# The first norm's rows loaded once and spread by products, scale ahead of shift, and two bias rows moved behind the experts

## The reference

```python
c_act = jax.nn.silu(c)
mod = c_act @ ada_w[l] + ada_b[l]                 # 1024 -> 6144
shift1, scale1, gate1, shift2, scale2, gate2 = jnp.split(mod, N_MOD, axis=-1)
h = modulate(rmsnorm(x, norm1_g[l]), shift1, scale1)   # h * (1 + scale) + shift
proj = h @ w_in[l]
...
out = peer(h2, ...)      # 128 gathered rows of each table for every token
...
p = h @ w_in_2 + b_in_2  # second block; the two gates' columns of b_in_2 are 1024 each
```

## Time and profile before

| | us |
|---|---|
| median of three runs | 1439.09 (1437.6 to 1442.28) |
| the profiled execution's own time | 1438.15 |
| its span | 1436.4 |
| PE busy | 1252.2 (87%) |
| DVE busy | 770.3 (54%) |
| POOL busy | 522.6 (36%) |
| ACT busy | 412.8 (29%) |

### The profile page before, as it was taken

The page is one execution under the profiler, slowest core; times in us unless marked ns, Lnnn a source line. Parts: engine busy times, 40 slices in busy tenths (PEclk is TensorE's granted clock), DMA queues, the critical chain, the costliest instruction groups (busy, mean ns, idle before and its releaser), DMA issues.

```text
span 1436.4 us, 13292 instructions
## 1 busy us (share of the span) xinstructions
PE 1252.2 (87%) x4187; PEld 653.2 (45%) x4187; DVE 770.3 (54%) x1584; ACT 412.8 (29%) x1106; POOL 522.6 (36%) x578
## 2 busy tenths in 40 slices
PE   3899879999777777777987777999999999999997
PEld 0486546555222222222543222654444446887443
DVE  1437258557356575878667678477996522110003
ACT  2122224334324343343434434322115211111000
POOL 1000036666457777777777777001111000000000
PEclk9899989999979999999999999999999999999999
DMA  9786369999999999999999999243334343434430
GB/s 352 269 299 234 117 222 391 406 406 408 401 403 409 410 409 410 409 407 406 409 402 407 405 406 405 85 162 117 117 118 155 110 158 118 176 129 164 163 129 29
DMA packets 131117, 399.85 MB, mean 278 GB/s; under 512 B 10328, under 2 KB 11480, under 8 KB 130664
## 3 DMA queue, kind: packets, MB, share of 16 engines
q0 software_dynamic: 74448, 271.09, 47.8%
q1 hardware_dynamic: 54448, 121.18, 23.4%
q10 hardware_dynamic: 2152, 6.74, 1.3%
HBM read 397.92 MB, written 1.05 MB: 278 GB/s over the span
## 4 chain that ended last, share of the span: by engine, by line
PE 48%; DMA 24%; DVE 9%; POOL 8%; issue 4%; DVEq 3%; ACT 2%; SPq 1%; ACTq 1%; POOLq 0%
PE psum L579 27%; DMA gathered<-in_peer_u_dram,expert_idx 20%; PE psum L1074 8%; PE psum L824 7%; POOL gathered L496 4%; POOL gathered L510 4%; DVE work L1494 3%; DMA gathered<-in_peer_v_dram,expert_idx 2%; DVE gathered L1831 2%; DMA gathered<-in_ada_w_dram 2%; PE psum L662 1%; PE psum L602 1%; DVE work L2116 1%; PE psum L1049 1%; SPq L426 1%
## 5 line engine op out<-in xcount | busy, mean ns | idle before, releaser
L824 PE MATMUL psum<-gathered,modr 128*128 128x512 f32 x1024 | 506.5, 627 | 127.1 <-DMA gathered<-in_peer_v_dram,expert_idx 104.8
L1831 DVE CUSTOM_DVE_ANT_0 gathered<-gathered,psum 128x1024 f32<-128x1024 f32 x256 | 312.1, 1219 | 173.2 <-DMA gathered<-in_peer_u_dram,expert_idx 171.1
L824 PEld LDWEIGHTS psum<-gathered,modr 128*128 128x128 f32 x1024 | 182.2, 194 | 431.7 <-DMA gathered<-in_peer_v_dram,expert_idx 249.1
L496 POOL DMA_INDIRECT gathered<-in_peer_u_dram,expert_idx x256 | 252.7, 987 | 312.1 <-DVE expert_idx L1502 182.3
L510 POOL DMA_INDIRECT gathered<-in_peer_v_dram,expert_idx x256 | 240.2, 938 | 85.1 <-issue 70.0
L579 PE MATMUL psum<-featT,weight_ring 128*128 128x256 f32 (+2 forms) x1280 | 221.5, 332 | 1.6 <-ACT featT L1112 1.4
L579 PEld LDWEIGHTS psum<-featT,weight_ring 128*128 128x128 f32 x1280 | 200.7, 194 | 32.0 <-issue 13.7
L579 PE MATMUL psum<-weight_ring,featT 128*128 128x512 f32 (+1 forms) x480 | 207.9, 588 | 2.4 <-ACT featT L1112 2.4
L1494 DVE TENSOR_TENSOR work<-work 128x1088 f32<-128x1088 f32 (+5 forms) x115 | 118.1, 1042 | 129.2 <-ACT work L1141 101.1
L579 PEld LDWEIGHTS psum<-weight_ring,featT 128*128 128x128 f32 x480 | 90.1, 192 | 108.4 <-issue 104.3
L1273 ACT ACTIVATE gel<-dots 128x1 f32<-128x1 f32 x256 | 51.3, 200 | 276.1 <-DVEq L1833 275.8
(11 more groups left out here) (283 smaller groups left out, 884.9 us busy)
## 6 DMA issues: line engine op xcount, KB each, us to landing
weight_ring<-in_w_in_dram SPq DMA_DIRECT2D x13, 2048.0 KB, 8.9
weight_ring<-in_ada_w_dram SPq DMA_DIRECT2D x11, 2048.0 KB, 17.2
weight_ring<-in_w_up_dram SPq DMA_DIRECT2D x8, 2048.0 KB, 8.8
weight_ring<-in_w_down_dram SPq DMA_DIRECT2D x8, 2048.0 KB, 7.8
weight_ring<-in_peer_wq_dram SPq DMA_DIRECT2D x4, 2048.0 KB, 14.7
gathered<-in_w_in_dram SPq DMA_DIRECT2D x2, 2048.0 KB, 12.9
gathered<-in_peer_u_dram,expert_idx POOLq DMA_INDIRECT x256, 11.2
gathered<-in_peer_v_dram,expert_idx POOLq DMA_INDIRECT x256, 11.2
```

The lines of the kernel that those rows point to most:

```text
L496: pool.indirect_dma_start(u_rows[:, slot, :], None, T["peer_u"], bass.IndirectOffsetOnAxis(ap=expert_idx[:, r % 2, k:k + 1], axis=0),).the ...
L824: mm = pe.matmul(psum[:, SUM_BANK + half, :], diag[:, e % 8, :], v_rows[:, slot, 512 * half:512 * (half + 1)], start=(e % EXPERTS == 0), s ...
L1831: dve.tensor_tensor_reduce(u_rows[:, slot, :], u_rows[:, slot, :], h2_rows[t], 1.0, 0.0, ALU.mult, ALU.add, dots[:, col:col + 1])
```

## The change

- The two broadcast loads of the head become loads of one row each (8 KB of `ada_b`, 4 KB of `norm1_g`) into partition 0, on the same queue and at the same places in its order.
- PE spreads them: after the first chunk's product, two products of one row (`ones[0:1, :]` by the `norm1_g` row) fill two PSUM banks, and DVE copies these 1024 columns to `A1`. Four more (`ada_bias`) write the bias into the four banks of the sums, and `ada_sum_on_bias(i)` adds its sum on top.
- The chunks come in the order 2, 3, 0, 1, so the scale is there first. DVE makes the gain of one half straight from PSUM, then that half of `x * rs * A1` for both tiles, then the same for the other half. When a shift bank is full, DVE adds that half from PSUM, for tile 0 and then for tile 1. `h1_ready` counts four halves, and PE's turns wait each for its own half.
- SP issues the bias rows GS0 and GM0 not while experts are gathered but with V0 and O0, behind the wait for `h0_ready`.

The diff, cut to these:

```diff
@@ plan
-    ada(0, 4)
+    ada(2, 4)
+    ada(0, 2)
@@ SP
                     sp.dma_start(bc_raw, T["s5_bc"]).then_inc(flag("in_bc"), 16)
-                    for i, lo in ((2, GS0), (3, GM0)):
-                        sp.dma_start(vec[:, D * i:D * (i + 1)], rowvec("b_in_2", lo, lo + D)).then_inc(
-                            flag("in_bias2"), 16)
                 if c == LAST_ADA + 4:
                     sp.wait_ge(flag("h0_ready"), TT)
-                    for i, lo in ((0, V0), (1, O0)):
+                    for i, lo in ((0, V0), (1, O0), (2, GS0), (3, GM0)):
@@ PE
-            ada(0)
-            for i in range(1, 4):
-                ada(i)
-                ada_sum(i - 1)
-            ada_sum(3)
+            def ada_bias(i):
+                pe.matmul(bank_of("ada", i), ones[0:1, :], modr[0:1, 512 * i:512 * (i + 1)],
+                          start=True, stop=False)
+            def ada_sum_on_bias(i):
+                turn_read_wait(pe, "ada", i, 0)
+                pe.matmul(bank_of("ada", i), quarter_rows[:, :], ada_part[:, i % 2, :], start=False,
+                          stop=True).then_inc(bank_full[GROUP_BANK[("ada", i)]], 1)
+            ada(2)
+            pe.wait_ge(flag("in_mod"), 32)
+            for half in range(2):
+                last = pe.matmul(psum[:, 6 + half, :], ones[0:1, :], A1[0:1, 512 * half:512 * (half + 1)],
+                                 start=True, stop=True)
+            last.then_inc(flag("gain_full"), 1)
+            for i in ADA_ORDER[:4]:
+                ada_bias(i)
+            ada(3)
+            ada_sum_on_bias(2)
+            ada(0)
+            ada_sum_on_bias(3)
+            ada(1)
+            ada_sum_on_bias(0)
+            ada_sum_on_bias(1)
...
+            def turn_h1(t):
+                for q in range(2):
+                    bank = begin_turn("h1", t, q)
+                    pe.wait_ge(flag("h1_ready"), TT * q + t + 1)
@@ ACT
-            load(modr[:, 0:2 * D], rowvec("ada_b", 0, 2 * D), "in_mod")
+            load(modr[0:1, 0:2 * D], T["ada_b"][0:2 * D].partition_broadcast(1), "in_mod")
             load(pos_i[:, :], T["positions"], "in_pos")
-            load(A1, rowvec("norm1_g", 0, D), "in_n1")
+            load(A1[0:1, :], T["norm1_g"][0:D].partition_broadcast(1), "in_mod")
@@ DVE
-            dve.wait_ge(flag("in_n1"), 16)
-            for i in range(4):
-                add_mod(i)
-                if i >= 2:
-                    dve.drain()
-                    sl = slice(512 * (i - 2), 512 * (i - 1))
-                    stt(A1[:, sl], scale1[:, sl], 1.0, A1[:, sl], ALU.add, ALU.mult)
+            dve.wait_ge(flag("gain_full"), 1)
+            dve.tensor_copy(A1, psum[:, 6:8, :].rearrange("p b n -> p (b n)"))
             dve.drain()
+            for half in range(2):
+                sl = slice(512 * half, 512 * (half + 1))
+                group_wait(dve, "ada", 2 + half)
+                read_out(stt(A1[:, sl], bank_of("ada", 2 + half), 1.0, A1[:, sl], ALU.add, ALU.mult),
+                         "ada", 2 + half)
+                dve.drain()
+                for t in range(TT):
+                    stt(hbuf[:, t, sl], xres[:, t, sl], rs[:, t:t + 1], A1[:, sl], ALU.mult, ALU.mult)
+            for half in range(2):
+                sl = slice(512 * half, 512 * (half + 1))
+                group_wait(dve, "ada", half)
+                dve.drain()
+                tt(hbuf[:, 0, sl], hbuf[:, 0, sl], bank_of("ada", half), ALU.add).then_inc(
+                    flag("h1_ready"), 1)
+                read_out(tt(hbuf[:, 1, sl], hbuf[:, 1, sl], bank_of("ada", half), ALU.add), "ada", half)
+                dve.drain().then_inc(flag("h1_ready"), 1)
-            for t in range(TT):
-                modulated(t, A1, shift1, "h1_ready")
```

More of the change, by code:

```diff
@@ L71 @@
 ADA_AT = {52: 10, 56: 11}
-ADA_ORDER = (0, 1, 2, 3, 4, 5, 8, 9, 6, 7, 10, 11)
+ADA_ORDER = (2, 3, 0, 1, 4, 5, 8, 9, 6, 7, 10, 11)
 PACK = [("c", KD), ("conv_w", 3 * CT), ("conv_g", CT), ("b_uqk", 12), ("qk_w", 32), ("qk_b", 8),
@@ L355, in build @@
             s5c[:, i, :] for i in range(15))
-        turns = [("ada", i, 0) for i in range(4)]
+        turns = [("ada", i, 0) for i in ADA_ORDER[:4]]
         turns += [("h1", t, q) for t in range(TT) for q in range(2)]
@@ L613, in _ @@
             pe.wait_ge(flag("consts"), 1)
+            def ada_bias(i):
[15 more added lines that the diff above has]
+            ada_sum_on_bias(2)
             ada(0)
-            for i in range(1, 4):
-                ada(i)
-                ada_sum(i - 1)
-            ada_sum(3)
+            ada_sum_on_bias(3)
+            ada(1)
+            ada_sum_on_bias(0)
+            ada_sum_on_bias(1)
             def tile_by_tile(name, src, ready, products, turn=None, before=None):
                 w = {}
-                units = 1 if turn else 2
+                units = 2
                 def tile(t):
@@ L669, in first_chunk @@
                         turn_read_wait(pe, name, 1, 1)
-            tile_by_tile("h1", hbuf, "h1_ready", [("q1", lambda t: t, 512), ("kv1", lambda t: t, 256)])
+            def turn_h1(t):
+                for q in range(2):
+                    bank = begin_turn("h1", t, q)
+                    pe.wait_ge(flag("h1_ready"), TT * q + t + 1)
+                    for j in range(4):
+                        k = 4 * q + j
+                        last = pe.transpose(bank[:, j * P:(j + 1) * P], hbuf[:, t, k * P:(k + 1) * P],
+                                            ident[:, :])
+                    last.then_inc(turned, 1)
+            tile_by_tile("h1", hbuf, "h1_ready", turn=turn_h1, products=[("q1", lambda t: t, 512), ("kv1", lambda t: t, 256)])
             def turn_rotated(t):
@@ L1546, in add_mod @@
                 group_wait(dve, "ada", i)
-                if i == 0:
-                    dve.wait_ge(flag("in_mod"), 16)
                 if i == 4:
```

## The result

The changed kernel takes 1425.87 us (median of 6 runs, 1423.99 to 1430.23) beside 1439.7 us of the kernel before in the same session (6 runs, 1437.6 to 1442.28): the ratio is 0.9904 with an interval of 0.9888 to 0.992. So it is faster, by 0.8 to 1.1%. The forecast was 1425.3 us with a range of 1421.5 to 1432.0, and the chance for "faster" was 0.9. A repeat in a later session, told at the end of the experiments, gave 1432.1 us, 0.1 us outside the range; what makes the kernel's own runs differ by so much is the most useful thing that this case showed.

The account below looks back on a forecast made before the run. The head was taken as bound by DMA bytes, then a serial stretch, and the experts by DMA. Terms 8.8 + 2.4 + 2.6 = 13.8 us off the median of 1439.1 gave 1425.3 us, range 1421.5 to 1432.0.

Parts of the forecast that it names:

- Bytes of the head: Head loads: 1.56 MB fewer at 389 GB/s land the last ada_w chunk 4.0 us earlier, at 29.2 us.
- rival 4: Head: row loads land late and PE waits; at 20.4 us, 3.9 us lost, 1429.2; chance 0.05, of slower 0.02.
- The serial stretch: Last chunk to first projection: only half-width shift additions remain on DVE; projection starts at 35.8, 8.8 us earlier including the bytes.
- The clock of the first projection: First projection product: all 16 records at the high clock take 6.9 us instead of 9.34, saving 2.4 us.
- rival 1: Head: PE's clock falls before the projection or rises late; price 2.4 us, 1427.7 us; chance 0.2.
- The bias rows: Experts: moving two 512 KB rows out of the full DMA stretch saves 2.6 us; behind it they are covered.
- What hides the six added products: PE in the head: they cost nothing, done at 28.1 us against a last landing at 29.2, 1.1 us of cover.
- four high: PE in the head: the four bias products run at the high clock, from 18.8 to 22.2 us.
- The rival of a late rise: Part of rival 1: clock rises only after the six products; PE free at 31.6 instead of 29.2, 2.4 us more.
- a sign: Head: the ada products start at about 11.7, 18, 23.5 and 29.2 us.

Follow-up runs that it names:

- the bytes back: Changed kernel with the two broadcast head loads sent to all 128 partitions again, products still reading one row: 1429.52 us, ratio 0.9935.
- the bytes alone: Kernel before with only the one-row loads and the six products that spread them, old chunk order and norm: 1437.68 us, ratio 0.9986.
- the head alone: Changed kernel with the two gate bias rows loaded again while experts are gathered: 1429.88 us, ratio 0.993.
- with them alone: Kernel before with only the two gate bias rows moved behind the experts: 1437.92 us, ratio 0.9986.
- the enlarged run: Changed kernel plus sixteen more loads of a 512 KB row (8.39 MB) during the experts, read by nobody: 1447.3 us, ratio 1.0052.
- the full rows with filler: Changed kernel with the six products over all 128 rows, plus five unread products ahead of the last ada product: 1423.48 us, ratio 0.9894.
- both kernels with early products and one-row products: Changed kernel plus five unread full-row products ahead of the first chunk: 1424.14 us; the same with the bias products spread, each before its sum: 1423.57 us.
- the kernel with both early products and filler: Changed kernel with the six products over 128 rows, plus five unread products ahead of the last ada product and five ahead of the first chunk: 1424.23 us.
- the kernel with early work: Changed kernel plus five unread products of 128 rows and 256 columns ahead of the first chunk: 1424.14 us, ratio 0.9907.
- the first full-row kernel: Changed kernel with the six products over all 128 rows, buffers zeroed first, no unread products added: 1426.49 us, ratio 0.9919.
- the kernel with spread bias products: Changed kernel plus five unread products ahead of the first chunk, with the four bias products spread, each before its sum: 1423.57 us, ratio 0.9903.

## Why the prediction was right, and which step wasn't

**Bytes of the head: right.** The last chunk lands at 29.4 us where 29.2 was forecast and 33.2 had been; with the bytes back it is 32.9. The row loads landed in time, and rival 4 fell.

**The serial stretch: right.** From the last `ada` to the first projection product 6.73 us (30.29 to 37.02) against 6.6 forecast (29.2 to 35.8) and 11.33 before. That this and the clock behind it are the larger part of the gain is shown from both sides: with the bytes back 7.2 of the 9.9 us stay, and the bytes alone bring 0.9 us in the median. The bytes' own term, 4.0 us at the landing, was worth 2.7 at the projection.

**The clock of the first projection: right in the profiled run, but not safe.** 6.97 us from its start to the next row instead of 9.34: 2.4 us, as forecast. The clock stayed at 1.00 although PE did nothing but two turns of transposes between 34.23 and 36.35 us. Nine of the ten profiles with the new order are like this. In the tenth, the head alone, the clock fell at about 41.7 us behind the same two turns and the same idle pieces, and cost 1.7 us (8.83 against 7.13). So what rival 1 feared happens in some runs. Rival 1 cites the Trainium skill, "TensorE: Matmul & The Clock Gate", section "Part 4: PE-mode transpose", for transposes that don't count as work; this one fall agrees with it, but doesn't tell the transposes from the idling between them.

**The bias rows: right.** 3.1 us between the gathers where 2.6 were forecast; 2.5 with them alone; 2.44 us for a MB in the enlarged run; and no reader waits for them.

**What hides the six added products: wrong.** This is the step that failed. I had the clock rise behind 7.1 us of PE's work, "four high" for the bias products, and 1.1 us of cover at the last chunk. Measured, the gain's products were already fast for the most part (1.96 us for four records), then the clock fell in the bias products, with PE never idle, and the next `ada` was slow too: PE is 0.9 us late rather than 1.1 early. With 0.2 us of later landing and 0.1 in the serial stretch that makes the projection 1.2 us later than forecast (37.02 against 35.8), and the head's gain 9.8 instead of 11.2 us at the first gather. The rival of a late rise was priced too low as well. I gave it 2.4 us, with the later `ada` products fast; in the repeat's profile the next `ada` ran slow as well and the projection started 5.0 us after 35.8. The starts of `ada` that the prediction lists as a sign (18 and 23.5 us for the second and third) also don't follow from its own working, which has them at 22.2 and 25.2; measured were 22.78 and 27.36.

So the closeness of the number is partly luck. The medians differ by 13.8 us, the very sum of the prediction, but the two profiled spans by 13.0: 1.4 less than forecast at the first gather, 0.5 more in the experts. And the six runs of the first session lie at 1424 to 1430, the repeat's six, of the same kernel, at 1427 to 1434.5; with these six the median is 6.8 us above the forecast. Of six profiles with one-row products and no early work, three show the clock up during the gain's products (the changed kernel, the one with more rows, the one with the bytes back) and three show it low until about 30 us (the head alone, the bytes alone, the repeat), with all instructions ahead of it at the same times to 0.3 us, but for the one with the bytes back. What decides between the two is open. Not all of the repeat's loss is this: of the 5.2 us between its span and the changed kernel's (1428.6 and 1423.4), 3.8 stand at the projection, 2.4 are left at the first gather, 2.8 at the last, and 2.4 come in the second block, where the clock dips at other places. One such dip lies ahead of the first gather, from about 156 to 163 us in the changed kernel: from projection to first gather it is 142.8 us in the changed kernel and 139.9 in the full rows with filler and in both kernels with early products and one-row products, in which there is no dip (141.4 in the kernel with both early products and filler, and in the repeat, where it is shorter). How much of the 2 us between their medians and the changed kernel's first is this dip, and whether the head's clock has a part in it, wasn't separated.

## What to carry to other kernels

Loading a row once and spreading it by a product saves bytes only if the product has cover at the low clock as well; price such fillers at both levels, and where one level costs something, look at several runs. A chunk that PE waits for is best met by PE arriving just in time and busy: too late costs the lateness, and too early can cost the clock: 2.40 us too early cost 1.5 us in one profile, 2.42 us nothing in another. In a stretch whose queue is full the price of a load is its bytes over the rate that the stretch shows, and moving it behind that stretch gives all of it back.

## What the hardware showed

A product of one row takes the time of one of 128 rows: with PE's clock up, four gain records take 1.82 us from start to next start with one row (14.31 to 16.13, with the early products) and 1.82 with 128 (14.57 to 16.39, full rows with early products and filler). The Trainium skill, "TensorE: Matmul & The Clock Gate", section "Why this matters for your kernels", says this of 32 rows; the trace agrees, down to one.

For the clock they aren't the same. With one row it fell in the middle of these products in the changed kernel (at 19.4 us) and in the kernel with early work, or never rose over the 10.5 us that twelve of them took (15.71 to 26.25 in the repeat), PE being without a gap each time. It was low for some part of them, or right behind them, in all eight profiles with one-row products. With 128 rows at the same place it never fell during these products or behind them while PE was busy, in three profiles of three. In the kernel with filler it was 1.00 from 18 to 36 us, with records at their fast spacing (3.52 us for eight), and from its first `ada` at 12.26 PE idles nowhere before 33.7 us:

```profile
20.00:26.00 6.00, 6.00 (x35) 1.83 (x37) 1.02 (x2) 0.58 (x1) 0.00 (x0) 1.00 1.05 387
```

A busy share of PE in the profile is therefore no sign that its clock stays up; the shape of the products counts as well. The rows that differ hold zeros, so it is the shape of the product and not its data that matters here. An idle piece of 2.40 us ahead of the last chunk was followed by a low clock in the first full-row kernel, one of 1.70 us in the kernel with spread bias products as well, but one of 2.42 us in the kernel before wasn't. The pieces of 0.86 and 0.67 us around the transposes weren't in nine profiles and were in one. So the length of an idle piece alone doesn't tell here what the clock does.
